# Parameters of the state-space part loaded as rows and turned on TensorE; the first tile, gain and query weights of the scores loaded during the output projection

## The reference

```
h = rmsnorm(x, norm1);  proj = h @ w_in
q, k, v, g, a_lr, u = split(proj)
o_gla = rmsnorm(gla(q, k, v, log_a)) * silu(g)
dt = exp(log_dt)                       # one for each of 32 groups
ab = exp((lam_re + i lam_im) * dt)     # 32 groups x 64 states
bb = f(lam, ab) * (b_re + i b_im)
y  = scan(ab, bb, u), read out with c_re, c_im, + d_skip * u
o_s5 = glu(gelu(y))
x = x + concat(o_gla, o_s5) @ w_out
h2 = rmsnorm(x, norm2)
q2 = h2 @ peer_wq                      # 8 heads, 2 halves of 128
s  = q2 . peer_keys                    # 128 keys for each half
... top 16 of each half, top 16 of 256 pairs, softmax,
... 128 experts a token: x = x + sum gate * gelu(u_e . h2) * v_e
y  = rmsnorm(x, final_norm)
```

## Time and profile before

| | |
|---|---|
| median of 3 runs | 3463.15 us (3463.12 to 3464.73) |
| the profiled execution | 3457.04 us, of which the span is 3455.3 us |
| mean granted TensorE clock | 0.975 |
| busy share of the span: PE, DVE, ACT, POOL | 95%, 74%, 26%, 23% |

### The profile page before, as it was taken

How to read it: one execution, slowest core, us unless ns; L and a number is a source line. 1 busy time by engine, 2 the same in 40 slices (tenths; PEclk the granted TensorE clock), 3 DMA queues, 4 the chain that set the end, 5 groups by cost and what they waited for, 6 DMA issues and landing times. The chain is left out here.

```text
span 3455.3 us, 46046 instructions
## 1 busy us (share of the span) xinstructions
PE 3269.0 (95%) x17804; PEld 2870.0 (83%) x17804; DVE 2551.4 (74%) x5345; ACT 910.8 (26%) x1319; POOL 800.3 (23%) x626
## 2 busy tenths in 40 slices
PE   6999989799999999989999999968999999999996
PEld 5867755499999999989999999966888888888884
DVE  4621253421499999988988898847899898998995
ACT  3210300211122222224444444411222222222222
POOL 0000000000001111113333333323344344443441
PEclk8999989899999999999999999988999999999998
DMA  3020021311144444448888889779888888888883
GB/s 96 14 39 27 13 92 55 116 44 43 62 133 145 146 139 145 146 157 289 294 320 295 327 290 334 277 274 316 301 299 303 301 298 298 299 305 301 300 294 128
DMA packets 339553, 695.58 MB, mean 201 GB/s; under 512 B 40956, under 2 KB 201528, under 8 KB 333176
## 3 DMA queue, kind: packets, MB, share of 16 engines
q1 hardware_dynamic: 255192, 386.29, 33.1%
q0 software_dynamic: 84144, 306.35, 26.0%
HBM read 580.11 MB, written 110.64 MB: 200 GB/s over the span
## 5 line engine op out<-in xcount | busy, mean ns | idle before, releaser
L1725 POOL DMA_INDIRECT dr_row<-in_peer_v_dram,idx x288 | 427.7, 1485 | 662.8 <-DVE acc_s L1744 636.5
L1725 POOL DMA_INDIRECT gr_row<-in_peer_u_dram,idx x240 | 290.5, 1210 | 482.1 <-DVE raw L1734 463.6
L1744 DVE SCALAR_TENSOR_TENSOR acc_s<-dr_row,gate,acc_s 128x1024 f32<-128x1024 f32 x288 | 367.2, 1275 | 0.0
L2271 DVE TENSOR_TENSOR acc<-pd_po,acc 128x512 f32<-128x512 f32 x384 | 264.0, 688 | 116.5 <-PE pd_po L2304 116.5
L1734 DVE CUSTOM_DVE_ANT_0 gr_row<-gr_row,xs 128x1024 f32<-128x1024 f32 x240 | 287.6, 1217 | 2.6 <-DMA gr_row<-in_peer_u_dram,idx 2.6
L2157 ACT ACTIVATE pg_wb<-pg_pw 128x512 f32<-128x512 f32 x192 | 207.9, 1102 | 51.7 <-PE pg_pw L2135 48.9
L476 PE MATMUL fr_a<-pj_w,h_t 128*128 128x256 f32 (+1 forms) x864 | 198.1, 391 | 16.2 <-PEq L176 16.2
L2108 DVE TENSOR_SCALAR pg_hot_i<-pg_iota,sel_t 128x128 f32<-128x128 f32 x768 | 212.9, 354 | 0.0
L476 PEld LDWEIGHTS fr_a<-pj_w,h_t 128*128 128x128 f32 (+1 forms) x864 | 170.1, 226 | 43.3 <-issue 21.4
L2135 PE MATMUL pg_pw<-pg_hot_i,pg_hot_j 128*128 128x128 f32 x1536 | 200.6, 276 | 3.0 <-DVE pg_hot_i L2108 3.0
L2135 PEld LDWEIGHTS pg_pw<-pg_hot_i,pg_hot_j 128*128 128x128 f32 x1536 | 192.7, 192 | 3.4 <-DVE pg_hot_i L2108 3.4
(11 more groups left out here) (479 smaller groups left out, 7935.2 us busy)
## 6 DMA issues: line engine op xcount, KB each, us to landing
pd_v<-in_peer_v_dram SPq DMA_DIRECT2D x128, 512.0 KB, 4.8
w_d<-pg_wb SPq DMA_DIRECT2D x48, 1024.0 KB
pd_w<-w_d SPq DMA_DIRECT2D x64, 768.0 KB, 7.1
pd_a<-act_d SPq DMA_DIRECT2D x64, 768.0 KB
ta_u<-in_peer_u_dram SPq DMA_DIRECT2D x64, 512.0 KB
ga_u<-in_peer_u_dram SPq DMA_DIRECT2D x64, 512.0 KB
act_d<-ta_a SPq DMA_DIRECT2D x128, 192.0 KB
act_d<-ga_a SPq DMA_DIRECT2D x128, 192.0 KB
```

What stands on the lines that cost most here:

```text
L1725: pool.indirect_dma_start(self.buf[i % self.n][:], None, self.table, bass.IndirectOffsetOnAxis(ap=self.idx[:, col:col + 1], axis=0)).then_ ...
L1744: self.nc.vector.scalar_tensor_tensor(out=out, in0=self.buf[i % self.n][:], scalar=w[:, col:col + 1], in1=out, op0=ALU.mult, op1=ALU.add). ...
L2271: nc.vector.tensor_tensor(out, po[(OUTS * g + o) % NPO][:], out, ALU.add).then_inc(o_added, 1)
```

## The change

`lam`, `log_dt` and `d` come as rows: 16 rows of 128 for each part of `lam`, 16 rows of 2, 32 rows of 16. They are issued behind the tiles of `x` and ahead of `pj_w`. VectorE widens the 16x2 of `log_dt` to 16x128, TensorE turns the four behind tile 7, and VectorE copies them to their places at the end of `norm1`. `b` and `c` are loaded as before.

A class `Lead` has a buffer of its own for tile 0 of the order, the gain and the first weight block. Its three loads are in SyncE's list of `gla_out`, behind the last load of `x` and ahead of the stores of the states. GpSimd doesn't wait for its stores at the end of `gla_out` any more; whoever reads `x2_d`, or writes over what a store still reads, waits for the store's semaphore. A memset of 128x2048 in `peer_scores` goes from the start to behind the last tile.

```diff
@@ class Params
+    def load_rows(self, queue, A, rows, loaded):
+        lam, ldt, dd = rows
+        for i, n in enumerate(("s5_lam_re", "s5_lam_im")):
+            queue.dma_start(lam[:, i], A[n][0].rearrange("(q h) p -> q (h p)", h=2)).then_inc(loaded, 16)
+        queue.dma_start(ldt[:], A["s5_log_dt"][0].rearrange("(q h) -> q h", h=2)).then_inc(loaded, 16)
+        queue.dma_start(dd[:], A["s5_d"][0].rearrange("(g c) -> g c", c=GCH)).then_inc(loaded, 16)
+
     def load(self, queue, A):
-        for i, n in enumerate(("s5_lam_re", "s5_lam_im")):
-            queue.dma_start(self.lam[:, i, :], A[n][0].rearrange("(q h) p -> (h p) q", h=2)).then_inc(self.loaded, 16)
-        for h in range(2):
-            queue.dma_start(self.ldt[ST * h:ST * h + ST, :],
-                            A["s5_log_dt"][0].rearrange("(q h) -> h q", h=2)[h:h + 1, :].broadcast_to([ST, GP])
-                            ).then_inc(self.loaded, 16)
         for i, n in enumerate(("s5_b_re", "s5_b_im")):
             queue.dma_start(self.bin[:, i], A[n][0].rearrange("(q h) p c -> (h p) q c", h=2)).then_inc(self.loaded, 16)
-        queue.dma_start(self.dd[:], A["s5_d"][0].rearrange("(g c) -> c g", c=GCH)).then_inc(self.loaded, 16)
@@ norm1, tensor
+                if t == NTP - 1:
+                    pe.wait_ge(rows_loaded, 16 * 4)
+                    pe.wait_ge(widened, 1)
+                    for i in range(2):
+                        nc.tensor.transpose(tq[:, i * GP:(i + 1) * GP], lam_r[:, i], ident[0:GP, 0:GP])
+                    nc.tensor.transpose(tq[:, 2 * GP:3 * GP], ldt_w[:].rearrange("q h p -> q (h p)"), ident[0:GP, 0:GP])
+                    nc.tensor.transpose(tq[0:GCH, 3 * GP:], dd_r[:], ident[0:G, 0:G]).then_inc(rows_turned, 1)
@@ norm1, vector
+                if t == NTP - 1:
+                    dve.wait_ge(rows_loaded, 16 * 4)
+                    nc.vector.tensor_copy(ldt_w[:], ldt_r[:].unsqueeze(2).broadcast_to([GP, 2, ST])).then_inc(widened, 1)
...
+            dve.wait_ge(rows_turned, 1)
+            nc.vector.tensor_copy(params.lam[:], tq[:, 0:2 * GP].rearrange("p (i q) -> p i q", i=2))
+            nc.vector.tensor_copy(params.ldt[:], tq[:, 2 * GP:3 * GP])
+            nc.vector.tensor_copy(params.dd[:], tq[0:GCH, 3 * GP:])
@@ gla_out, gpsimd
                 pool.dma_start(x2_tiles[t], x[t % 3][0:rows(t)]).then_inc(stored[t % 3], 16)
-            for b in range(3):
-                pool.wait_ge(stored[b], 16 * (NT // 3))
@@ class Lead
+    def in_memory(self, engine, t):
+        engine.wait_ge(self.stored[t % 3], 16 * (t // 3 + 1))
+
+    def load(self, sp, x2_tiles):
+        self.in_memory(sp, ORDER[0])
+        sp.dma_start(self.x, x2_tiles[ORDER[0]]).then_inc(self.x_in, 16)
+        sp.dma_start(self.wide, self.gain.rearrange("(o d) -> o d", o=1).broadcast_to([P, D])).then_inc(self.wide_in, 16)
+        sp.dma_start(self.raw, wq_block(self.wq, 0)).then_inc(self.w_in, 16)
@@ peer_scores, sync
-            load_x(0)
-            sp.dma_start(wide, gain.rearrange("(o d) -> o d", o=1).broadcast_to([P, D])).then_inc(wide_loaded, 16)
-            load_w(0)
             load_x(1)
+            load_x(2)
             load_w(1)
-            load_x(2)
             load_x(3)
+            load_x(4)
             sp.dma_start(keys_sb, keys.rearrange("h s n d -> n (h s) d")).then_inc(keys_loaded, 16)
-            for s in range(NX, NT):
+            for s in range(NX + 1, NT):
                 load_x(s)
@@ peer_scores, vector
-            nc.vector.memset(s_sb[:, NT - 1], 0.0).then_inc(cleared, 1)
             dve.wait_ge(rooted, 1)
-            dve.wait_ge(wide_loaded, 16)
+            dve.wait_ge(lead.wide_in, 16)
...
             low_tile(NT - 1)
+            nc.vector.memset(s_sb[:, NT - 1], 0.0).then_inc(cleared, 1)
```

59 lines of the change are left out of this document (45 added, 14 removed).

## The result

| | median us | lowest to highest | executions |
|---|---|---|---|
| before, beside the changed kernel | 3463.14 | 3461.55 to 3464.73 | 4 |
| changed | 3436.64 | 3431.37 to 3444.86 | 4 |

The ratio is 0.9926 (95% interval 0.9904 to 0.9947): 26.5 us faster. The sign held, and so did the mechanism at `front` and at weight block 1; the price of GpSimd's drain and the time from which the gain was subtracted didn't. Note the third column: the executions of the changed kernel lie 13.5 us apart, those of before only 3.2 us. Most of what follows is about that.

A forecast was written before the change was run, and what follows sets the result against it. TensorE, 95% busy, was taken to idle before `front` behind `log_dt`'s slow load and at the step to `peer_scores`; 14.6 + 1.9 + 3.0 = 19.5 us off 3463.15 gave 3443.6 us, range 3438.5 to 3451.

The forecast's parts named there:

- What bounds the kernel: TensorE, busy 95%, idles 16.2 us before `front` because one DMA engine works through `log_dt`; second idle stretch at `peer_scores`.
- Part 1: End of `norm1`: with parameters as rows, SyncE is ready before the compute; `front` starts at 31.3, 14.6 us earlier.
- Part 2, the barrier: End of `gla_out`: without the store wait, GpSimd's 0.80 us drain ends sooner; 1.9 us gained, bounds 0 and 2.5.
- Part 2, block 1: Start of `peer_scores`: weight block 1, now third load, lands at 8.0 us; low weights 1 start 3.0 us sooner.
- The sum: Whole kernel: 14.6 + 1.9 + 3.0 = 19.5 us gained.
- The base: Whole kernel: the gain is subtracted from the median of before, 3463.15 us, with 2 us at either side.
- Everything after 700 us is rigid: Stages after 700 us keep their lengths, so everything later shifts by 19 to 20 us.
- `s_bin` by itself: Rival, loads in `norm1`: `s_bin` is slow itself and its stall stays; gain 16.8 us, 3446.4 us; chance 0.08.
- The step gives less: Rival, step to `peer_scores`: drain waits for the store or block 1 lands fourth; 1.5 to 3 us, 3446-3447; chance 0.12.
- the shift is lost before the experts' stage: Rival, from `front` on: another wait takes most back or the shift is lost; gain 4.9 to 8 us; chance 0.05.
- The slower clock: Rival, `front`: TensorE stays at its lower clock; over 39 us of it cancels the gain, 60 gives 3473.7; chance 0.02.
- the sign that was named for it: Sign of a wrong forecast, in `front`: TensorE's clock at 0.5 for more than 4 us, against some 2.5 expected.

The follow-up runs named there:

- both kernels on `log_dt`: Before with `log_dt` loaded in one DMA of contiguous values: 3444.77 us; the changed kernel with `log_dt` alone loaded as before: 3451.72 us.
- the wide load: Kernel before with `log_dt` alone altered: one DMA copying its 32 contiguous values to each of 128 partitions; 3444.77 us, ratio 0.9950.
- paused: Changed kernel with the eight TensorE pauses of the experts' first stage lengthened by VectorE writing 704 columns of zeros; 3448.09 us, ratio 0.9969.
- store_sp: Changed kernel with the last of the nine stores at the end of `gla_out` issued by SyncE instead of GpSimd; 3441.27 us, ratio 0.9947.
- filled pair: Before and the changed kernel, each with unused TensorE transposes filling the pauses of the experts' first stage; 3455.67 and 3436.31 us.
- again2: Changed kernel run a third time, nothing altered; 3436.51 us, ratio 0.9933.
- before2: Kernel before, unaltered, profiled a second time; 3462.79 us, ratio 1.0003.
- before_filled: Kernel before with unused TensorE transposes added in the eight pauses of the experts' first stage; 3455.67 us, ratio 0.9991.
- filled: Changed kernel with unused TensorE transposes added in the eight pauses of the experts' first stage; 3436.31 us, ratio 0.9935.

## Why the prediction was wrong

**What bounds the kernel: right.** The stall before `front` was `log_dt`, worked off at the DMA share of one engine, with SyncE blocked behind it; both kernels on `log_dt` show it.

**Part 1: right in mechanism and size.** Over 11 profiles with the rows or the wide load (paused left out here, and below where the work behind the projection is compared) `front` starts at 31.1 us on average (29.2 to 32.5), over the five without at 46.1: 14.9 us, forecast 14.6. The first profile alone, at 30.3, looked like more. Its clock was up again before `front` began, and its `u` pieces took 34.48 us instead of 35.84; but the whole way from the start of `front` to its last projection piece is 394.3 to 398.4 us without the change (mean 396.9) and 396.3 to 400.5 with it (397.3). Nothing of that is kept on average, as the prediction assumed.

**Part 2, the barrier: the term that failed.** 0.6 us instead of 1.9 in all ten profiles where GpSimd isn't made to wait and issues the last store. The drain ends 0.4 us behind the store's landing whether or not anybody waits for it. I had taken the drain's 0.80 us as a fixed price, though that row was read where the store had already landed. A drain measured behind a wait for the same transfer tells nothing of a drain without that wait. The bound of 2.5 us, with ScalarE's end deciding, is what store_sp reached: 4.5 less 1.8 is 2.7.

**Part 2, block 1: right.** From SyncE's first issue to the projection it takes 19.6 to 19.8 us before and 15.9 to 17.8 in the nine profiles with the unaltered lead, mean 16.7: 3.0 us, as forecast. Block 1 lands at 7.1 to 9.0 us, not always at 7.1.

**The sum.** By the marks 14.9 + 0.6 + 3.0 = 18.5 us, forecast 19.5. The filled pair measured 19.4. The terms together promised 1 us too much, so they can't be what put the result below the range.

**The base: failed.** The prediction subtracted from 3463.15 us, the median of three executions that happened to lie within 1.6 us, and gave 2 us at either side for it. 89 executions of before lie between 3451.3 and 3468.7 around 3460.0. From there the same sum gives 3440.5, still 3.9 us above what was measured, and the range, moved by as much, 3435.4 to 3447.9, holds the result. So this is the step that put it outside: 3.1 of the 6.9 us. The before beside the changed kernel gave the same high 3463.14, which is why the 26.5 us of the result look so large; beside two other sets of runs of before the same kernel gains 23.2 and 21.7. The 2 us for the median were too few as well: 15 executions of the changed kernel have a standard deviation of 5.0 us, so that a median of four is uncertain by more than that.

**"Everything after 700 us is rigid": failed in single executions.** The same work from the first projection with block 1 to the last store took from 2765.3 to 2776.3 us. In the first profile of the changed kernel it took 2766.3, in that of before 2774.6, and this 8.3 us is what looked like an unexplained gain. On average it is 2772.9 in the five profiles with `front` at 46 us and 2771.0 in the eleven, 1.9 us apart with a standard error of 1.9. The prediction put this term at nothing, and on average the profiles don't contradict it. The forecast was also set against a median although the profile of before had run 6.1 us below it, so this spread was there to be read.

**What stays open.** The 15 executions of the changed kernel have a median of 3436.5 us, 23.5 below before's 3460.0; the means are as far apart, with a standard error near 1.4 us. The marks say 18.5 and the filled pair 19.4, the latter with a standard error of 1.6. No mark shows the other 4 us, which are some two standard errors. It may be that the clock is low for less time in the changed kernel's later stages. The falls counted in the experts' first stage (one, three, three with `front` at 46; three, none, none, three, three, none, three, none at 29 to 33) don't tell it from chance, and the profiles lose as much to the clock behind the projection with `front` early as late (46.9 and 47.4 us on average). An estimate from the mean granted clock of every execution leans that way: (1 - clock) x span is 88.2 us on average over the 85 executions of before that have it on record and 76.0 over the 15 of the changed kernel, 12.2 less; up to the projection the profiles show 9.3 of it (38.7 in the three of before and before_filled, 29.4 in the four of the changed kernel and filled). The 3 us left over have a standard error above 2.

**The rivals.** `s_bin` by itself is refuted. "The step gives less" came true in its mechanism at the drain, at a price of 1.3 us. That the shift is lost before the experts' stage is refuted: at the first projection the four profiles of the changed kernel and filled are 18.5 us ahead of the three of before and before_filled. The slower clock didn't come as a loss, since `front`'s length is unchanged on average. But the sign that was named for it, a clock at 0.5 for over 4 us of `front`, shows in again2 (5.4 us), and with `front` late it shows in before2 too (5.2 us): the prediction took 2.5 us to the rise, plus or minus 1, from one profile, and over all 18 it is 0 to 5.7.

## What to carry to other kernels

A long DMA issue can be the price of the load ahead of it: read the DMA share of that stretch and the landing times before blaming the name in the row. Where a wait for a transfer is taken away, ask what the engine does next, since a drain behind it may wait for the same transfer. And before a forecast of a few tenths of a per cent, find out how far executions of the unchanged kernel lie apart, and subtract from a median of many. Three profiles of the changed kernel agree to 1.0 us at the start of `front`, to 3.6 at the first projection and only to 14.2 at the last store.
